# Routing in fewer operations, a second block begun inside the first, earlier turns at the end, and a second attention step with its exponentials ahead of copies

## The reference, cut to what matters

```python
group_prob = softmax(t @ w_group + b_group); gp, gi = top_k(group_prob, 1)
in_group = logits of the 4 experts of group gi; ev, ei = top_k(in_group, 2)
ew = softmax(ev) * gp
for e in range(16):
    he = silu(t @ w_gate[e]) * (t @ w_up[e])
    y = y + gates[:, e:e+1] * (he @ w_down[e])
return rms_norm(h + y)
```

## Time and profile before

| what | us |
|---|---|
| median of three runs (1173.19 to 1180.81) | 1175.32 |
| the profiled execution | 1176.15 |
| its span, first to last instruction | 1174.4 |
| PE busy in the span | 1063.8 (91%) |
| DVE busy | 829.8 (71%) |
| ACT busy | 641.4 (55%) |
| POOL busy | 468.4 (40%) |

### The profile page before, as it was taken

One profiled execution on the slowest core, in us unless ns is written; L12 is line 12 of the kernel. 1 busy time (PEld: TensorE's weight loads), 2 busy tenths in 40 slices (PEclk: granted clock), 3 DMA queues, 4 the chain that ended last, 5 costly groups with the idle time before them and its releaser, 6 DMA issues. The chain is left out here.

```text
span 1174.4 us, 21278 instructions
## 1 busy us (share of the span) xinstructions
PE 1063.8 (91%) x7138; PEld 895.0 (76%) x7138; DVE 829.8 (71%) x1218; ACT 641.4 (55%) x1008; POOL 468.4 (40%) x303
## 2 busy tenths in 40 slices
PE   5899989999987988999999927999999999999997
PEld 4898978989976746666666716888888888878875
DVE  4797856655248556465555378888989888888996
ACT  5522111155542348354454325888888888878874
POOL 1121211121100126211111213778877987878970
PEclk9999989899997999999999967999999999999999
DMA  7215334342033560001112484999699999763445
GB/s 271 70 60 73 104 100 124 108 116 83 21 63 84 194 208 2 1 37 55 54 55 72 145 339 131 398 379 296 223 375 377 395 297 372 236 183 76 123 121 220
DMA packets 89494, 194.98 MB, mean 166 GB/s; under 512 B 9264, under 2 KB 32048, under 8 KB 88768
## 3 DMA queue, kind: packets, MB, share of 16 engines
q1 hardware_dynamic: 82800, 169.92, 41.3%
q0 software_dynamic: 6624, 24.12, 8.5%
HBM read 157.69 MB, written 31.51 MB: 161 GB/s over the span
## 5 line engine op out<-in xcount | busy, mean ns | idle before, releaser
L2301 PE MATMUL ps<-weights_higher,split 128*128 128x512 f32 x1152 | 315.1, 395 | 3.0 <-DVE split L2501 2.3
L2301 PEld LDWEIGHTS ps<-weights_higher,split 128*128 128x128 f32 x1152 | 214.1, 189 | 46.1 <-issue 2.6
L489 PE MATMUL ps<-xsplit,wsplit 128*128 128x384 f32 (+2 forms) x1440 | 243.2, 327 | 3.2 <-POOL wsplit L261 3.2
L489 PEld LDWEIGHTS ps<-xsplit,wsplit 128*128 128x128 f32 x1440 | 229.8, 192 | 4.3 <-POOL wsplit L261 3.5
L2347 ACT CAST weights_higher<-gate_up 128x1024 fp32r (+1 forms) x192 | 200.1, 1054 | 53.0 <-PE ps L2301 49.3
L2423 DVE TENSOR_TENSOR weights_lower<-gate_up,weights_higher 128x1024 fp32r<-128x1024 f32 x144 | 179.2, 1291 | 14.0 <-ACT weights_higher L2347 12.2
L2301 PE MATMUL ps<-weights_lower,split 128*128 128x512 f32 x576 | 178.7, 392 | 1.8 <-DVE weights_lower L2423 1.8
L261 POOL TENSOR_TENSOR wsplit<-mem,wsplit 128x1024 fp32r<-128x1024 f32 x22 | 55.5, 2523 | 253.1 <-ACT wsplit L344 253.1
L2241 POOL TENSOR_TENSOR weights_lower<-gate_up,weights_higher 128x1024 fp32r<-128x1024 f32 x48 | 120.1, 2502 | 78.1 <-ACT weights_higher L2347 77.1
L2301 PEld LDWEIGHTS ps<-weights_lower,split 128*128 128x128 f32 x576 | 108.5, 189 | 26.0 <-DVE weights_lower L2423 2.6
L2423 DVE TENSOR_TENSOR weights_lower<-weights,weights_higher 128x1024 fp32r<-128x1024 f32 x72 | 110.3, 1583 | 25.3 <-ACT weights_higher L2347 25.3
(11 more groups left out here) (431 smaller groups left out, 1782.1 us busy)
## 6 DMA issues: line engine op xcount, KB each, us to landing
weights<-in_w_down SPq DMA_DIRECT2D x16, 2048.0 KB, 15.3
gate_up<-in_w_gate SPq DMA_DIRECT2D x30, 1024.0 KB
gate_up<-in_w_up SPq DMA_DIRECT2D x30, 1024.0 KB
mem<-in_w_in SPq DMA_DIRECT2D x22, 512.0 KB, 4.2
mem<-in_x SPq DMA_DIRECT2D x10, 512.0 KB, 3.7
mem<-in_w_out SPq DMA_DIRECT2D x1, 4096.0 KB, 15.6
h_d<-mem SPq DMA_DIRECT2D x8, 512.0 KB, 2.6
xn_d<-mem SPq DMA_DIRECT2D x8, 512.0 KB, 2.6
```

The source lines that it names most:

```text
L489: mm = nc.tensor.matmul(ps[:, n % 6, 0:hi - lo], w[slot_of(h)][:, k % 4, P * m:P * m + P], x[:, k, lo:hi], start=(k == 0 and p_ == 0), sto ...
L2301: mm = nc.tensor.matmul(ps[:, bank + h, :], x, w[place % RING][:, 512 * h:512 * h + 512], start=(k == 0 and p_ == 0), stop=(k == n - 1 and ...
```

## The change

It has four parts.

- **Routing in fewer operations.** The logits of each tile get norm and bias in one operation (`dve_logits`), six tiles of them inside the attention's steps 17 to 37, the last two at the start of `dve_route`. The group's maximum goes by three operations, and the two best experts by a rank: all pairwise differences of the group's four logits, compared with a small tie constant (`C_TIE`), summed; rank below 2 gives `OKB` at once, ranks 0 and 1 the one-hot rows afterwards. Block counts and slots take fewer operations. The iota that `HOTR` is compared with is copied by ACT to SBUF (`IOTAH`). The tables of experts and places are made from 128 partitions' columns by three small matmuls (`ROWS`). The first weight chunk is no longer lowered inside the chain; the shares' six operations come behind the tables (`dve_slot_shares`), the second exponential behind ACT's first four chunks (`act_second_gap`). POOL's first two gathers take their indices from `ixb` directly and stand ahead of its first weight chunk.
- **Second block begun inside the first.** PE starts block 0 with half of its rows copied, turns block 1's rows behind chunk 4, makes the slots' weights behind chunk 6, and turns block 0's hidden rows between chunks 1 and 2 of block 1. DVE makes the hot tables for the slots' weights one at a time between its chunks; ACT loads the silu table right behind block 0's rows.
- **Last two blocks.** The hidden rows of the last block are turned before the last down chunk of the block before it, copied into buffers of their own (`HH_LAST`, `HLO_LAST`), by ACT behind its second chunk and by DVE behind its first. ACT scales the outputs of the block before (`scale_outputs`), DVE makes only the lower parts (`lower_outputs_of`). One of the two token tables is made a block earlier; `OHT` has a new place.
- **Second attention step.** ACT's "t" pieces of step 1 come behind its exponentials.

The diff, cut to its core:

```diff
@@ act_attention
-                    while r < len(ring) and ring[r][0] == "t" and step_of(*ring[r][:2]) <= n:
+                    while n > 1 and r < len(ring) and ring[r][0] == "t" and step_of(*ring[r][:2]) <= n:
@@ dve_attention, new
+                if n >= 17 and n % 4 == 1:
+                    dve_logits(dve, link, (n - 17) // 4)
+        def dve_logits(dve, link, p):
+            t = tile_of(p)
+            dve.wait_ge(ring_free, [r for r, v in enumerate(ring) if v[0] == "s" and v[1] == p][0] + 1)
+            link(nc.vector.scalar_tensor_tensor(LGR[:, t], LGR[:, t], RS2[:, t:t + 1], BR, ALU.mult, ALU.add))
@@ dve_route
+            link(red(GM, gl, AX.X, ALU.max))
             tt(GX, gl, b4(GM), ALU.subtract).then_inc(gaps_ready, 1)
+            dve.wait_ge(gaps_ready, 3)
+            link(stt(VAL, GX, 0.0, desc, ALU.is_equal, ALU.mult))
+            link(red(MX, VAL, AX.X, ALU.max))
+            link(tt(OHG, VAL, b4(MX), ALU.is_equal))
...
+            link(tt(DIFF, IG.unsqueeze(2).to_broadcast(s44), IG.unsqueeze(3).to_broadcast(s44), ALU.subtract))
...
+            link(red(RANK, DIFF, AX.X, ALU.add))
+            link(ts(VAL, RANK, 2.0, None, ALU.is_lt))
...
-            dve_weights_lower(dve, None, 0, "gu", 0, 0)
...
             for k in range(2):
                 tt(HOTR[:, NT * k:NT * k + NT], fl[0][:, NT * k:NT * k + NT].to_broadcast([P, NT, P]),
-                   IOTAP.unsqueeze(1).to_broadcast([P, NT, P]), ALU.is_equal).then_inc(slot_hot_ready, 1)
+                   IOTAH.unsqueeze(1).to_broadcast([P, NT, P]), ALU.is_equal).then_inc(slot_hot_ready, 1)
...
+            tt(COLS[:, 2:3], EVEN, ODD, ALU.subtract).then_inc(slot_hot_ready, 1)
+            for k in range(RING - 1):
+                dve_weights_lower(dve, None, k, "gu", k, 0)
...
+            nc.vector.tensor_copy(dtab[0:1], ROWS[:, 2]).then_inc(tables_ready, 1)
@@ pool_experts
+            pool.wait_ge(slots_ready, 1)
+            for b in range(2):
+                pool.sem_inc(ix_seen, 1)
+                pool.indirect_dma_start(XG[:, b], None, xn_d, bass.IndirectOffsetOnAxis(ap=ixb[:, b:b + 1], axis=0)).then_inc(xg_loaded[b], 16)
             lower(None, RING - 1, "gu", RING - 1, 0)
-            pool.wait_ge(slots_ready, 1)
-            gather(0, 0)
-            gather(1, 1)
@@ pe_experts
                 for k in range(KD):
+                    if turn is None and k == 0:
+                        pe.wait_ge(xh_ready, 1)
+                    if turn is None and k == KD // 2:
+                        pe.wait_ge(xl_ready, 2)
                     product(turn, k, k, KD, XH[:, par, k], XL[:, par, k], 2 * par)
+                    if turn is None and k == KD // 2:
+                        turn_x(0, 1)
+                    if turn is None and k == KD - 2:
+                        pe_slot_weights(pe)
+                    if turn_inside and k == 1:
+                        turn_hidden(turn)
...
                     if kind == "down":
-                        product(b, place, k, FF // P, HH[:, k], HLO[:, k], 0 if par and last else 4)
+                        if last and not par and k == FF // P - 1:
+                            turn_hidden(b + 1)
+                        product(b, place, k, FF // P, hi[:, k], lo[:, k], 0 if final else 4)
@@ act_experts
-            act.wait_ge(slots_ready, 1)
+            act_second_gap(act)
             copy_x(0, 0)
+            nc.scalar.activation(SD2[:, 0:1], con[:, C_ONES:C_ONES + 1], ACT.Silu)
             for k in range(RING, KD):
                 higher(None, k, "gu", k, 0)
+            copy_x(1, 1)
...
-                    if place == RING - 1:
+                    if place == (1 if par and last else RING if first and not par else RING - 1):
...
+                if par and last:
+                    scale_outputs(b - 1, 0, 4, False)
@@ dve_experts
+            dve_slot_shares(dve, link)
+            dve_rows_lower(dve, 0, 0)
+            dve_slot_parts(dve, link)
+            dve_slot_hot(dve, link, 0)
+            lower(None, RING, "gu", RING, 0)
+            dve_slot_hot(dve, link, 1)
+            for k in range(RING + 1, KD - 1):
+                lower(None, k, "gu", k, 0)
+            dve_slot_hot(dve, link, 2)
+            x_lower(1, 1)
...
+                    if place == KD and last and not par:
+                        tokens_of_slots(b, 0)
...
+                    if par and last:
+                        if place == 0:
+                            hidden_lower(b, HH_LAST, HLO_LAST)
+                        if place == RING - 1:
+                            lower_outputs_of(b - 1, 0, b + 1)
```

More of the change, by code:

```diff
@@ L58 @@
 P_END = 64 + 1024
-MEM = 48432
+MEM = 48416
 HALF_W = 4 * 256
@@ L1903, in act_route, with act_second_gap @@
             act.wait_ge(gaps_ready, 3)
-            nc.scalar.activation(GX, GX, ACT.Exp).then_inc(rt_exp, 1)
+            nc.scalar.activation(GE, GX, ACT.Exp).then_inc(rt_exp, 1)
+            act.wait_ge(rank_done, 1)
+            nc.scalar.activation(IOTAH, IOTAP, ACT.Identity, bias=con[:, C_OFF:C_OFF + 1])
+            nc.scalar.copy(IOTAS, IOTAP).then_inc(rt_exp, 1)
+        def act_second_gap(act):
             act.wait_ge(gaps_ready, 4)
@@ L1927, in pe_route @@
             mm.then_inc(idx_done, 1)
+            pe.wait_ge(slot_hot_ready, 3)
+            for i in range(3):
+                mm = nc.tensor.matmul(ROWS[:, i], COLS[:, i:i + 1], ident[:, 0:NB], start=True, stop=True)
+            mm.then_inc(idx_done, 1)
         def pe_slot_weights(pe):
-            pe.wait_ge(slot_hot_ready, 3)
+            pe.wait_ge(slot_hot_ready, 4)
             for n in range(2 * NT):
@@ L2083, in build @@
         SG, HE = take(FF), take(FF)
+        assert oS <= O_LAST and O_LAST + 2 * FF <= oC
+        HH_LAST, HLO_LAST = (LAST_T[:, FF * i:FF * i + FF].rearrange("p (k q) -> p k q", k=FF // P) for i in range(2))
         XG = con[:, C_COS:C_COS + 2 * D].rearrange("p (b n) -> p b n", b=2)
@@ L2317, in pe_experts @@
             gate_up(0, 0, None)
-            turn_x(0, 1)
-            pe_slot_weights(pe)
             def body(j, par, first, last):
                 b = 2 * j + par
-                pe.wait_ge(he_ready, b + 1)
-                pe.wait_ge(xl_ready, 2 * b + (4 if has(par, last, 1) else 2))
-                for k in range(FF // P):
-                    mm = nc.tensor.transpose(ps[:, 6, P * k:P * k + P], HE[:, P * k:P * k + P], ident)
-                mm.then_inc(het_ready, 1)
-                if has(par, last, 1):
-                    gate_up(b + 1, 1 - par, b)
+                final = par and last
+                if not final:
+                    pe.wait_ge(xl_ready, 2 * b + 4)
+                    if par or not first:
+                        turn_hidden(b)
+                    gate_up(b + 1, 1 - par, b, first and not par)
                 pe.wait_ge(hl_ready, b + 1)
@@ L2332, in body @@
                     turn_x(j + 1, par)
-                if (par or not first) and not (par and last):
+                if (par or not first) and not final:
                     pe.wait_ge(ye_copied, 2 * b)
-                for place, (kind, k) in enumerate(chunks(not has(par, last, 1))):
+                hi, lo = (HH_LAST, HLO_LAST) if final else (HH, HLO)
+                for place, (kind, k) in enumerate(chunks(final)):
                     if kind == "down":
-                        product(b, place, k, FF // P, HH[:, k], HLO[:, k], 0 if par and last else 4)
+                        if last and not par and k == FF // P - 1:
+                            turn_hidden(b + 1)
+                        product(b, place, k, FF // P, hi[:, k], lo[:, k], 0 if final else 4)
             return blocks(pe, body)
@@ L2405, in body @@
                     higher(b, place, kind, k, q_next if kind == "gu" else q)
-                    if place == RING - 1:
+                    if place == (1 if par and last else RING if first and not par else RING - 1):
                         act.wait_ge(het_ready, b + 1)
-                        nc.scalar.copy(HH, ps[:, 6, :].rearrange("p (k q) -> p k q", k=4)).then_inc(hh_ready, 1)
+                        nc.scalar.copy(HH_LAST if par and last else HH, ps[:, 6, :].rearrange("p (k q) -> p k q", k=4)).then_inc(hh_ready, 1)
                 if has(par, last, 1):
@@ L2496, in body @@
                         lower(b, place, kind, k, q_next if kind == "gu" else q)
-                    if place == RING - 1:
-                        if (par or not first) and not (par and last):
+                    if par and last:
[3 more added lines that the diff above has]
+                            lower_outputs_of(b - 1, 0, b + 1)
+                    elif place == (RING if first and not par else RING - 1):
+                        if par or not first:
                             outputs_of(b - 1, 1 - par, first)
-                        dve.wait_ge(hh_ready, b + 1)
```

(4 more changed lines are left out.)

195 lines of the change are left out of this document (95 added, 100 removed).

## The result

The changed kernel took 1164.96 us (median, 1163.44 to 1167.65) where the kernel before took 1175.32: ratio 0.9918, 95% interval 0.9893 to 0.9944. That is 10.4 us less where 14.1 were forecast. It lies inside the range given and clear of no change, but within 1% of it, where 0.73 of the chance had stood on more than that.

The account below looks back on a forecast made before the run. TensorE (PE) was taken as the bound nearly throughout, with gains only where it waits. Terms 4.0 + 5.8 + 0.65 - 0.35 - 0.3 + 2.1 + 2.2 = 14.1 off 1175.32 gave 1161.2 us, range 1157.6 to 1167.

Parts of the forecast that it names:

- more than two waits for `weights_lower`: Sign of being wrong: PE waiting more than twice for DVE's lower weight parts among the expert blocks.
- the gather under 5.5 us: Sign of being right: the first gather of token rows after routing takes less than 5.5 us.
- Attention: Second attention step: exponentials first remove 2.57 us of PE idle and half-clock logits; 4.0 us, bounds 2.6 and 4.2.
- Slots: Routing: DVE's shorter chain of operations has the slots ready at 696.9 instead of 702.43, 5.5 us sooner.
- the collision that the prediction saw in 1.99: Routing: one DVE operation took 1.99 us, elsewhere 0.29, while POOL ran a 1024-wide subtraction; moving that removes it.
- Gather: After routing: the first gather lands at 702.8 instead of 708.62, 5.8 us sooner including the slots' 5.5.
- the alone row: The old first gather's 4.90 us, without loads beside it; the median of all 24, mostly beside loads, was 6.9.
- rival (a): Early stages gain less: gather at 704.4, rows' lower half behind a collision, clock falling in attention; all three 4.4 us; chance 0.15.
- First block: Expert start: 0.65 from an earlier start, minus 0.35 clock and 0.3 collision, plus 2.1 from removing the hidden-rows wait.
- Rival (c): Expert blocks: waits for the scatter stall every second block, 11 x 1.8 = 20 us, giving 1181; chance 0.03.
- The end: Last blocks: earlier turn and token table let the final sums begin at 1144.1, before 1146.28; 2.2 us.
- Rival (b): Tail: final sums wait for the residual rows' load, so 2.2 us is lost, giving 1163.4; chance 0.08.

Follow-up runs that it names:

- e1: Changed kernel with only the second attention step's old order, copies ahead of exponentials; ratio 0.9972 to the kernel before.
- e8: e6 with both of the last pair's token tables at the very end; median 1160.82 us, ratio 0.9861 to the kernel before.
- e9: Changed kernel with the first block's hidden rows turned ahead of the second block's products again; ratio 0.993 to the kernel before.
- e7: Changed kernel with POOL's subtraction ahead of the two first gathers again; ratio 0.9912 to the kernel before.
- e3: Changed kernel with the first expert's down weights loaded behind the first gather's landing; ratio 0.9893 to the kernel before.
- e2: Changed kernel with both token tables at the end of the last block; ratio 0.9891 to the kernel before.
- e4: Changed kernel with the first token table made right behind the last block's hidden rows; ratio 0.9896 to the kernel before.
- e6: e4 with scatter a third of a block sooner, first down weights loaded behind the gather, first rows lowered before slot shares; ratio 0.9863 to the kernel before.

## Why the prediction was right or wrong

The likeliest case was right in kind and 5.1 us too good by the traces: 14.1 forecast, 9.0 measured, of which 1.06 is from a stretch that wasn't changed; so the change's own part is 7.9. That the time fell inside the range is in part luck: the untouched stretch, attention and the first block came out 3.1 better than forecast, and the slots, the gather, the blocks and the end 8.2 worse. The median's 10.4 is more than the traces' 9.0 within the spread of single executions. Of the prediction's own signs of being wrong one came, more than two waits for `weights_lower` (four among the blocks); of its signs of being right the gather under 5.5 us didn't.

- **Attention: right** (4.4, and 4.7 by e1, forecast 4.0). The wait and the clock both went. The lower bound of 2.6, "if the clock falls all the same", is real too: it came in two of ten traces, e8 and e9.
- **Slots: right** (5.4, forecast 5.5), and the collision that the prediction saw in 1.99 is confirmed by e7.
- **Gather: wrong.** The step that failed is "I take 702.8, nearest to the alone row as the overlap is short". The gather took the loaded row's 6.9 and not 5.3, and issue and landing together lost 1.71 where 0.3 was to be won. e3 shows the cause, e7 what it means. This was rival (a), one part of three. The rule of the Trainium skill that the prediction quoted (DMA: Bandwidth & Descriptors, Queues, rings and completion order) had the right sign, and the delay of 0.75 worked out from it, an estimate, was still too small: 6.89 is 1.99 more than 4.90.
- **First block: better** (3.76, forecast 2.1). The wait of 2.10 went, and e9 shows that the turn's new place did it. The step by which the start came nearer to the landing was 0.85 (forecast 0.65). The 0.3 charged for a collision cost nothing there: no wait for the rows' lower half stands in the trace. The term "if so again, 0.65 us more of the block is at half speed: 0.35 back" had the wrong sign: the first three chunks took 5.71 from the first product and not 6.72. The 0.68 of idle between transposes and products had gone, and the clock rose 5 us behind the transposes, not 8.
- **Blocks: wrong.** Rival (c) was given 0.03 for all blocks and nothing for one or two: "the pattern moves as a whole". It doesn't: with the second block some 3.5 us sooner the loads fall otherwise against the scatter (6.2 to 6.7 us ahead of it, not 9.5 or more), and block four stalls, which it doesn't in e9. In the nine traces with the late scatter a single wait for it of up to 1.57 cost 0.1 at most, one of 1.62 to 1.72 cost 0.1 twice and 1.9 twice, and each from 1.85 on cost 1.8 to 3.6. Before, the twelve waits of the earlier trace rows held one of 2.26 and, one by one in DVE's timeline, others of 1.62, 1.39, 1.05 and 1.03: the pattern stood near its edge. That was the place to look. Why the wait at the eighteenth block was 3.31 in this trace and 2.0 to 2.5 in the six like it is not settled.
- **The end: wrong.** The failed step is "The earlier token table falls where DVE waited for ACT". It does, but POOL's subtraction falls there too, and the wait was 1.4 where table and collision took 3.6. The trace of the kernel before had both in the same place:

```profile
1128.45 2.41 POOL L2241 TENSOR_TENSOR weights_lower<-gate_up,weights_higher 128x1024 fp32r<-128x1024 f32 x1
...
1129.72 4.49 DVE L2423 TENSOR_TENSOR weights_lower<-weights,weights_higher 128x1024 fp32r<-128x1024 f32 x3 [1.34 <-ACT weights_higher L2347]
```

With both tables at the end, e2 gets 1.0 of the forecast 2.2; e4's place between is no better. Rival (b) didn't come: nothing waits for the residual rows.

The Trainium skill (GPSIMD Engine Reference, Specifications) says that VectorE's two-input operations and those of its two-port mode contend with GpSimd for an SBUF interface. The row of 2.32 agrees, as the scan reads two tensors. The row of 2.38 agrees if that operation, with one tensor and a scalar, ran in two-port mode, which no row here shows. The table there names no size; weighed at the token table, the rule would have spoken against that step.

## What to carry to other kernels

Before moving an operation into an engine's idle gap, look at what the neighbour on the shared path does in that gap: a small operation of DVE can cost the whole remainder of POOL's large one. Before counting on a shorter chain, ask what its transfer meets when it starts sooner; here 2 of the 5.4 us bought nothing. And a wait that costs next to nothing today (eleven of the twelve before, 0.4 to 1.6 us each) is a margin: list such waits with the value from which they bite, and move the transfer behind them (here the scatter, a third of a block sooner, 6 us) before anything that shifts their phase.

## What the runs showed of the hardware

- DVE on 8 or 16 numbers in each partition took 2.38 and 2.32 us while POOL ran a 1024-wide subtraction, 0.22 and 0.19 otherwise; three 1024-wide weights took 5.6 to 5.7 instead of 3.5.
- The first gather took 4.6 to 4.9 us from issue to landing where the loads were past or nearly so (before, e3, e6, e7, e8) and 6.5 to 7.0 beside loads at some 400 GB/s. The scatter took 9.4 to 12.1 us where DVE waited for it.
- After the same 1.45 us of PE idle at 430 us the logits took 2.02 us in eight traces and 3.58 and 3.52 in e9 and e8, with a granted clock of 0.70 and 0.57 in 432 to 436 (1.00 in e7), a mean over 1.2 and 2.4 GHz. No edit of these two touches that place; what decided it is open.
